# A decoder layer with expert retrieval: branches, first norm and scores by halves of the tokens, the second half laid between the gather slots of the first

## The chip, the cores and the metric

The kernel runs on one core of one Trainium2 chip. The metric is the device time of one execution in microseconds (us); a smaller time is better. The engines are PE (TensorE: matmuls, and its weight loads PEld), DVE (VectorE), ACT (ScalarE), POOL (GpSimd) and SP (SyncE, which here only issues DMAs). Sixteen DMA engines move data between DRAM and SBUF.

## What is computed

A decoder layer on 1024 tokens of width 1024. Cut to what matters here:

```python
h = x @ w_in                                   # q, k, v, p (pool, 512 wide), g (gates, 2048 wide)
o = rms_norm(diff_attention(q, k, v))          # 8 heads
attn_branch = o @ w_attn_proj
pooled = trailing_means(p) - p                 # windows 2, 4, 8, 16 along the tokens
pool_branch = (pooled @ pool_w * pool_scale) @ w_pool_proj
g_attn, g_pool = split(sigmoid(g + b_gate))
mix = (g_attn * attn_branch + g_pool * pool_branch) @ w_out
y = layer_norm(ALPHA * x + mix)
s = einsum(y @ peer_wq, sub_keys)              # 8 heads x 2 halves x 128 keys
top16 of each half, top16 of the 256 sums, idx = row * 128 + col, gate = softmax
act = gelu(u[idx] . y);  ffn = sum(gate * act * v[idx])     # 128 experts for each token
out = layer_norm(ALPHA * y + ffn)
```

Each token fetches 128 rows of u and v, chosen by its own scores: 1024 x 128 rows of 8 KB, 1.07 GB in all.

## The kernel before

Four stages follow one another, each closed by a barrier: `build_attention`, `build_branches`, `build_first_norm`, `build_peer`.

*Attention* (unchanged) leaves `xT_hi` and `xT_lo` (x turned, as a rounded part and the rest; every product of the first three stages is made of three fp32r matmuls of such parts) and `oT` in SBUF.

*Branches.* 20 blocks of `w_in` (4 for the pool branch, 16 for the gates) are loaded one by one. ACT makes the high part of a weight (L659), POOL the low part (L636), PE does two groups of 24 matmuls of 512 columns (one for each half of the tokens), ACT takes each out of PSUM (L671, or with the sigmoid L686). DVE does the pool branch's window sums for all 1024 tokens. Then 8 blocks of `w_branch` (ACT L699, POOL L647) are multiplied with `oT` and the pool result, 72 matmuls a block, and DVE gates and adds them (L768, L773, L778).

*First norm.* `w_out` is loaded and split (ACT L931, DVE L961), then 8 tiles of 128 tokens: 48 matmuls, residual and statistics on DVE (L971, L975), the power on POOL (L914), scaling on ACT (L936), gain and offset on DVE (L986, L988), store of y to DRAM, and 8 transposes into `yT`.

*Retrieval.* PE first multiplies query weights and keys into `km` (L1405), once for all tokens. The scores of a tile are then 32 plain fp32 matmuls (L1413). A tile has 128 **slots**, one gathered row for each of the 128 tokens: POOL issues the indirect DMA into a ring of 8 buffers (L1138), after PE has used the buffer's last content; DVE multiplies the u half with y and sums (L1364); ACT makes the gelu, the coefficient and a diagonal matrix, for a pair of slots at a time (L1183, L1187, L1193, 4 diagonal buffers); PE adds the v half by two fp32 matmuls (L1424). Beside the slots run the search of the head two ahead on DVE (`retrieve`, in 17 steps, `STEPS_AT` says how many at which slot), PE's scores of the next tile (one matmul each second slot, slots 17 to 79), and the last norm of the tile before. Each engine's order is written out by hand; DMAs queue on SP in program order.

Of the kernel before, what the change touches and what calls it, by code (L numbers as in the profile page):

```python
# [6 lines left out]

# [565 lines left out]

def build_branches(nc, ctx, w_in, pool_w, pool_scale, b_gate, w_branch, xT, oT, merged):
    at = Place(nc)
    pad = [at(f"pad{i}", 96 + 5 * i, [P, PAD + T]) for i in range(3)]
    pooled = [at(f"pooled{s}", 111 + 4 * s, [P, T], F32R) for s in range(2)]
    pw_raw = at("pw_raw", 119, [P, PG, P])
    pw = [at(f"pw{s}", 121 + 2 * s, [P, PG, P], F32R) for s in range(2)]
    count = at("count", 125, [P, PAD])  # L580
    icount = at("icount", 125.25, [P, PAD], I32)
    gates = at("gates", 96, [P, 2 * DC, T])
    pm_all = at("pm", 160, [P, PG, T])
    pm = [at("pm_hi", 32, [P, PG, T], F32R), at("pm_lo", 160, [P, PG, T], F32R)]
# [128 lines left out]
    def _(dve):  # L713
# [7 lines left out]
        for g, window in enumerate(WINDOWS):  # L721
# [7 lines left out]
            if g:  # L729
                dve.wait_ge(pooled_hi, g)  # L730
# [762 lines left out]
```

## Time and profile before

| | us |
|---|---|
| median of 3 runs | 3882.21 (3880.28 to 3883.63) |
| the profiled execution, whole time | 3879.75 |
| its span, first to last instruction | 3877.9 |
| attention | 0 to 667 |
| branches | 667 to 1070 |
| first norm | 1070 to 1184 |
| `km`, first scores, first searches | 1184 to 1257.6 |
| gathers issued | 1257.6 to 3848 |

The share of busy time of an engine is a mean over stages with different limits, so it is read by stage. A row of the grouped instructions gives their count, busy time, mean duration and the idle time before them. A row of the chain of waits names what the end was waiting for at that time. Matmul records of plain fp32 come in two for each instruction.

### The profile page before, as it was taken

To read this page: it belongs to the slowest core of one execution; us is meant where nothing else is said; L and a number is where in the kernel's file an instruction comes from. 1 tells how busy PE (TensorE), PEld (TensorE's weight loads), DVE (VectorE), ACT (ScalarE), POOL (GpSimd) and SP (SyncE) were. 2 spreads that over 40 slices of the span, in tenths; PEclk is the share of its full clock that TensorE was granted. 3 is DMA by queue.
4 is the path that set the end of the run, shared out by engine and by line. 5 is a ranking of instruction groups with operands and counts; after the bars stand their busy time and mean duration, and the time that the engine had idled before them with its cause. 6 is when DMAs were issued, how large, how long until landed. Compare 5 with 4: busy or idle time off the path is not lost.

```text
span 3877.9 us, 34466 instructions
## 1 busy us (share of the span) xinstructions
PE 3182.2 (82%) x9592; PEld 1687.1 (44%) x9592; DVE 2309.9 (60%) x5793; ACT 1233.1 (32%) x3644; POOL 1313.6 (34%) x1262
## 2 busy tenths in 40 slices
PE   7888886898987897788788788778878877877776
PEld 5767664687875333233233233323323323332222
DVE  4555555302252766766666667676677666767764
ACT  2333333222032333333333333333333333333332
POOL 2122111122200434444444444444444444444442
PEclk9989896999999999999999999999999999999999
DMA  2000000111034999999999999999999999999997
GB/s 83 17 23 22 22 11 9 42 46 48 32 130 132 409 421 421 420 419 414 418 418 417 419 414 419 414 415 417 415 415 417 416 415 416 419 416 415 413 417 331
DMA packets 166191, 1142.02 MB, mean 294 GB/s; under 512 B 19344, under 2 KB 19344, under 8 KB 34832
## 3 DMA queue, kind: packets, MB, share of 16 engines
q0 software_dynamic: 147456, 1073.81, 67.0%
q1 hardware_dynamic: 17856, 66.34, 5.0%
q8 instruction: 53, 0.87, 0.1%
q14 instruction: 106, 0.87, 0.1%
q10 hardware_dynamic: 720, 0.13, 0.0%
HBM read 1131.82 MB, written 8.39 MB: 294 GB/s over the span
## 4 chain that ended last, share of the span: by engine, by line
DMA 45%; PE 14%; DVE 5%; issue 3%; ACT 3%; POOL 0%; SPq 0%; POOLq 0%; ACTq 0%; DVEq 0%
DMA ring<-uv,idx 44%; PE r_o L1424 12%; DVE ring L1364 4%; ACT diag L1193 1%; DMA wq<-wqT 1%; PE r_s L1413 1%; ACT gel L1183 1%; ACT coef L1187 1%; PE r_s L1405 1%; POOL ring L1138 0%; DVE yn_e L1342 0%; DVE yn_e L1338 0%; DVE dot L1364 0%; DVE topi L1237 0%; DVE s L1238 0%
## 5 line engine op out<-in xcount | busy, mean ns | idle before, releaser
L1424 PE MATMUL r_o<-ring,diag 128*128 128x512 f32 x4096 | 1914.4, 611 | 492.8 <-ACT diag L1193 467.0
L1364 DVE CUSTOM_DVE_ANT_0 ring<-ring,ytok 128x1024 f32<-128x1024 f32 x1024 | 1253.7, 1224 | 774.0 <-DMA ring<-uv,idx 771.3
L1138 POOL DMA_INDIRECT ring<-uv,idx x1024 | 1083.4, 1058 | 1573.5 <-PE r_o L1424 1455.6
L1424 PEld LDWEIGHTS r_o<-ring,diag 128*128 128x128 f32 x4096 | 746.0, 192 | 1661.3 <-ACT diag L1193 861.7
L1183 ACT ACTIVATE gel<-dot 128x2 f32<-128x2 f32 x512 | 104.1, 203 | 1723.2 <-DVE dot L1364 1723.2
L1193 ACT ACTIVATE diag<-ident,coef 128x128 f32<-128x128 f32 x1024 | 347.4, 386 | 0.0
L66 PE MATMUL j_ps<-xT_hi,wa 128*128 128x512 f32 x768 | 258.4, 409 | 18.5 <-DVE xT_lo L354 18.5
L1413 PE MATMUL r_s<-km,yT 128*128 128x512 f32 x512 | 256.5, 592 | 0.8 <-ACT km L1155 0.8
L1187 ACT ACTIVATE coef<-gel,gate 128x1 f32<-128x1 f32 x1024 | 245.9, 287 | 16.8
L66 PE MATMUL b_ps<-xT_hi,wb 128*128 128x512 f32 x640 | 200.0, 393 | 12.8 <-POOL wb L636 10.1
L249 POOL TENSOR_SCALAR st_a<-st_a 128x1 f32<-128x1 f32 x64 | 12.2, 191 | 487.8 <-ACT sq L304 487.8
L66 PEld LDWEIGHTS j_ps<-xT_hi,wa 128*128 128x128 f32 x768 | 150.0, 195 | 60.6 <-issue 20.0
L66 PE MATMUL j_ps<-xT_lo,wa 128*128 128x512 f32 x384 | 154.9, 403 | 0.0
L316 ACT ACTIVATE e<-e,st_a 128x256 f32<-128x256 f32 (+7 forms) x128 | 98.3, 769 | 169.3 <-DVE st_a L430 169.3
L1413 PEld LDWEIGHTS r_s<-km,yT 128*128 128x128 f32 x512 | 97.2, 190 | 122.9 <-issue 121.9
L66 PEld LDWEIGHTS b_ps<-xT_hi,wb 128*128 128x128 f32 x640 | 121.8, 190 | 39.2 <-POOL wb L636 10.3
L66 PE MATMUL s_ps<-k,q 64*128 64x512 f32 (+2 forms) x576 | 109.1, 408 | 26.3 <-DVE st_a L425 26.2
L66 PE MATMUL b_ps<-xT_lo,wb 128*128 128x512 f32 x320 | 125.7, 393 | 0.0
L755 DVE TENSOR_TENSOR oT_lo<-oT,oT_hi 128x1024 fp32r<-128x1024 f32 x8 | 11.5, 1504 | 180.7 <-ACT oT_hi L703 180.7
L636 POOL TENSOR_TENSOR wb<-wb_raw,wb 128x1024 fp32r<-128x1024 f32 x20 | 48.2, 2410 | 187.0 <-ACT wb L659 187.0
L425 DVE CUSTOM_DVE_ANT_0 e<-s_ps,bias 128x512 f32<-128x512 f32 (+2 forms) x192 | 98.8, 553 | 7.0 <-DVE bias L413 2.7
L541 PE MATMUL o_ps<-v,aT 128*128 128x256 f32 x576 | 96.8, 323 | 3.2 <-DVE aT L400 3.2
(164 smaller groups left out, 2953.7 us busy)
## 6 DMA issues: line engine op xcount, KB each, us to landing
ring<-uv,idx POOLq DMA_INDIRECT x1024
wa_raw<-w_in SPq DMA_DIRECT2D x24, 512.0 KB, 3.6
wb_raw<-w_in SPq DMA_DIRECT2D x20, 512.0 KB, 3.6
wq<-wqT SPq DMA_DIRECT2D x16, 512.0 KB, 3.7
wc_raw<-w_branch SPq DMA_DIRECT2D x8, 768.0 KB, 4.2
x_raw<-xT SPq DMA_DIRECT2D x8, 512.0 KB, 9.5
wo_raw<-w_out SPq DMA_DIRECT2D x8, 512.0 KB, 7.4
xs<-x SPq DMA_DIRECT2D x8, 512.0 KB, 3.6
```

Source lines behind the costliest of these rows:

```text
L66: ins = nc.tensor.matmul(out, l(lhs[a]), r(rhs[b]), start=first and n == 0, stop=last and n == 3 * len(pairs) - 1)
L316: nc.scalar.activation(e[:, wh, 0:KEYS[s]], e[:, wh, 0:KEYS[s]], ACT.Exp, bias=nmx[:, wh:wh + 1], accum_out=den[:, wh:wh + 1]).then_inc(e_ ...
L425: nc.vector.tensor_tensor_reduce(e[:, wh, c * HALF:c * HALF + n], s_ps[i % 3][:, 0:n], bias[:, start:start + n], SCALE, -3.0e38, ALU.add, ...
L541: ins = nc.tensor.matmul(o_ps[:], part[:, i_a % 2, b * P:(b + 1) * P], v_both[u if tile >= 0 else 1 - u][:, :, 4 * c + b, :], start=c == 0 ...
L636: nc.gpsimd.tensor_tensor(w[r][1][:], w_raw[:], w[r][0][:].bitcast(F32), ALU.subtract).then_inc(w_split, 1)
L1138: nc.gpsimd.indirect_dma_start(out=ring[t % RING][:], out_offset=None, in_=uv, in_offset=bass.IndirectOffsetOnAxis(ap=idx[:, slot:slot + 1 ...
L1183: nc.scalar.activation(gel[:, slot:slot + GROUP], dot[:, slot:slot + GROUP], ACT.Gelu).then_inc(gelu_out, 1)
L1187: nc.scalar.activation(coef[:, slot + j:slot + j + 1], gel[:, slot + j:slot + j + 1], ACT.Copy, scale=gate[:, h, e:e + 1]).then_inc(coef_r ...
L1193: nc.scalar.activation(diag[(t + j) % DIAGS][:], ident[:], ACT.Copy, scale=coef[:, slot + j:slot + j + 1]).then_inc(diag_ready, 1)
L1364: nc.vector.tensor_tensor_reduce(ring[r][:, 0:D], ring[r][:, 0:D], ytok[n % 2][:], 1.0, 0.0, ALU.mult, ALU.add, dot[:, slot:slot + 1]).the ...
L1413: ins = nc.tensor.matmul(s_ps[b][:], yT[:, c, n * P:(n + 1) * P], km[:, c, b * HALF:(b + 1) * HALF], start=c == 0, stop=c == DC - 1)
L1424: ins = nc.tensor.matmul(o_ps[n % 2][half][:], diag[t % DIAGS][:], ring[t % RING][:, D + half * HALF:D + (half + 1) * HALF], start=slot == ...
```

## The change

After attention, everything is one block, `build_rest`, and everything between attention and retrieval is done for 512 tokens at a time (`stage(g)`, g = 0, 1) by smaller buffers. Stage 0 runs ahead of the gathers. Stage 1 is woven into the slots of tiles 0 to 3: after slot t every engine calls `advance(t)`, which emits those pieces of stage 1 whose number is at most t. The numbers:

```diff
+BASES = (-4000, 88)
+T_X, T_UNIT, UNIT_LEN = 0, 16, 6
+T_O = T_UNIT + UNIT_LEN * UNITS + 1
+T_BRANCH, BRANCH_LEN = T_O + 14, 8
+T_W = T_BRANCH + BRANCH_LEN * DC + 1
+T_NORM, NORM_LEN = T_W + 12, 12
+T_SCORE, HEAD_LEN = T_NORM + NORM_LEN * (GT + 1) + 4, 16
+def score_at(g, h):
+    if g == 0:
+        return HEAD_LEN * h - 62
+    return BASES[g] + T_SCORE + HEAD_LEN * h
```

So stage 1 loads its x at slot 88, does 20 units (a block of `w_in` times 512 tokens, 24 matmuls, 6 slots each) in slots 104 to 223, the 8 branch blocks (36 matmuls, 8 slots each) in 239 to 302, `w_out` from 304, four norm tiles (48 matmuls, 12 slots each) from 316, and its scores, a head each 16 slots, from 380 to 508. Of stage 0's scores the first 3.9 heads stand ahead of slot 0, the others in slots 2 to 66.

The scores no longer use `km`: queries are made for 512 tokens (8 fp32 matmuls of 512 columns for each of the 16 half heads), then compared with the keys (4 matmuls of 128 columns). They are stored to DRAM (`s_scr`, 512 KB a head) and read back by tile and head (128 KB, 64 times). `oT` goes through DRAM too (`o_scr`), x is loaded and split again for each half, and all weights of the stages (`w_in` blocks, `w_branch`, `w_out`, keys, query weights) are loaded twice. `w`, `wc` and the query weights have two buffers each, `mt`, `xs` and `zn` one.

The waits that the prediction speaks of:

```diff
+        def load_unit(g, i):                        # SP
+            u = UNITS * g + i
+            if u >= 2:
+                sp.wait_ge(unit, u - 1)
+            sp.dma_start(w_raw[u % 2][:], a["w_in"][FIRST_BLOCK + i]).then_inc(w_in[u % 2], 16)
...
+            def high(i):                            # ACT
+                u = UNITS * g + i
+                act.wait_ge(w_in[u % 2], 16 * (u // 2 + 1))
+                nc.scalar.activation(w[u % 2][0][:], w_raw[u % 2][:], ACT.Copy).then_inc(w_hi, 1)
...
+                yield unit_at(g, i + 1)
+                act.wait_ge(unit, u + 1)
...
+                    nc.scalar.activation(gates[:, j], ps[u % 2][:], ACT.Sigmoid, bias=bg[:, j:j + 1]).then_inc(evac, 1)
+                if i + 2 < UNITS:
+                    yield unit_at(g, i + 1) + 1
+                    high(i + 2)
...
+                yield branch_at(g, n + 1)           # DVE
+                dve.wait_ge(c_unit, 2 * c + 2)
+                nc.vector.tensor_tensor(gates[:, n + DC], gates[:, n + DC], ps[2 * (c % 2) + 1][:],
+                                        ALU.mult).then_inc(gated, 1)
...
+            if slot % TOPK == 13 and k + 3 < RH * TT:   # SP: s_scr to SBUF
+                search_in(k + 3)
```

**ACT, between two slot pairs of a gate unit.** Before, the rows of a slot pair stand alone (`gel`, two `coef`, two `diag`):

```order
L1193 ACTIVATE diag_6745<-ident,coef 128x128 [waits r_summed,r_coef_ready]
L1183 ACTIVATE gel<-dot 128x2 [waits r_dotted]
L1187 ACTIVATE coef<-gel,gate 128x1 [waits r_gelu_out]
L1187 ACTIVATE coef<-gel,gate 128x1
L1193 ACTIVATE diag_6742<-ident,coef 128x128 [waits r_summed,r_coef_ready]
L1193 ACTIVATE diag_6743<-ident,coef 128x128 [waits r_summed,r_coef_ready]
```

In the change, a sigmoid out of PSUM, the high part of a weight and two table loads stand between two pairs (slot 104 + 6k and the next one, then the pair behind):

```order
L1084 ACTIVATE diag_4931<-ident,coef 128x128 [waits r_summed,r_coef_ready]
L961 ACT_TABLE_LOAD
L961 ACTIVATE gates<-w_ps,bg 128x512 [waits r_unit]
L943 ACTIVATE wb_4870<-wb_raw_4861 128x1024 [waits r_w_in0]
L1074 ACT_TABLE_LOAD [waits r_gate_ready]
L1074 ACTIVATE gel<-dot 128x2 [waits r_dotted]
L1078 ACTIVATE coef<-gel,gate 128x1 [waits r_gelu_out]
L1078 ACTIVATE coef<-gel,gate 128x1
L1084 ACTIVATE diag_4928<-ident,coef 128x128 [waits r_summed,r_coef_ready]
```

The diagonals of the next pair now stand behind the wait for a weight load (`r_w_in0`).

**PE, slots of tile 0.** Before, one score matmul follows each second slot (two `r_o` rows are a slot):

```order
L1424 MATMUL r_o<-ring_6727,diag_6742 128x512 [waits r_diag_ready]
L1424 MATMUL r_o<-ring_6727,diag_6742 128x512
L1424 MATMUL r_o<-ring_6728,diag_6743 128x512 [waits r_diag_ready]
L1424 MATMUL r_o<-ring_6728,diag_6743 128x512
L1413 MATMUL r_s<-km,yT 128x512
```

In the change, where one unit ends and the next begins, three or six fp32r matmuls (`w_ps`) follow each slot:

```order
L1428 MATMUL w_ps<-xh,wb_4872 128x512
L1428 MATMUL w_ps<-xl,wb_4872 128x512
L1428 MATMUL w_ps<-xh,wb_4873 128x512
L1553 MATMUL r_o<-ring_4912,diag_4928 128x512 [waits r_diag_ready]
L1553 MATMUL r_o<-ring_4912,diag_4928 128x512
L1428 MATMUL w_ps<-xh,wb_4870 128x512 [waits r_evac,r_w_split]
L1428 MATMUL w_ps<-xl,wb_4870 128x512
L1428 MATMUL w_ps<-xh,wb_4871 128x512
L1428 MATMUL w_ps<-xh,wb_4870 128x512
L1428 MATMUL w_ps<-xl,wb_4870 128x512
L1428 MATMUL w_ps<-xh,wb_4871 128x512
L1553 MATMUL r_o<-ring_4913,diag_4929 128x512 [waits r_diag_ready]
```

The next unit's weights must be split by the slot at which the last unit ends.

**DVE, where a branch block ends (slot 255).** The rows of before have nothing between products (`ring,dot`) but search steps. In the change the gating stands between them:

```order
L1389 ISA ring_4919,dot<-ring_4919,ytok_4939 128x1024 [waits r_row_in7]
L1389 ISA dot 128x1
L1333 TENSOR_SCALAR gate<-gate,esum 128x16 [waits r_inverted]
L1192 TENSOR_TENSOR gates<-gates,w_ps 128x512 [waits r_c_unit]
L1389 ISA ring_4912,dot<-ring_4912,ytok_4938 128x1024 [waits r_row_in0,r_y_in0]
```

The product of slot 256 now stands behind the end of PE's work of slot 254.

## Rows read from the trace of the kernel before

**Rows 1.** The page: busy time by engine, and the DMA share in 40 slices.

```profile
PE 3182.2 (82%) x9592; PEld 1687.1 (44%) x9592; DVE 2309.9 (60%) x5793; ACT 1233.1 (32%) x3644; POOL 1313.6 (34%) x1262
...
DMA  2000000111034999999999999999999999999997
```

**Rows 2.** Windows: us, busy us of PE, PEld, DVE, ACT, POOL (instructions), PEclk, DMA, GB/s.

```profile
743.00:926.00 183.00, 177.49 (x774) 146.54 (x774) 2.27 (x2) 49.78 (x60) 36.10 (x15) 0.98 0.13 42
...
1070.00:1184.00 114.00, 99.19 (x448) 80.34 (x448) 63.12 (x88) 34.91 (x40) 4.49 (x9) 0.93 0.33 120
...
2300.00:2600.00 300.00, 245.32 (x532) 96.54 (x530) 206.62 (x524) 98.04 (x328) 125.90 (x119) 0.99 1.01 415
```

**Rows 3.** The chain of waits in the gathers: start us, us, what.

```profile
1240.10 27.75 PE r_s L1413 x64
...
1300.38 13.59 DMA ring<-uv,idx
1316.33 3.71 PE r_o L1424 x8
```

**Rows 4.** Source rows of the gathers: duration ns min/median/max, first and last start us.

```profile
L1138 POOL DMA_INDIRECT ring<-uv,idx x1024: 932/944/1997, 1257.6 to 3847.8; - x171
```

**Rows 5.** DMA issues: KB each, median us from issue to landing.

```profile
wb_raw<-w_in SPq DMA_DIRECT2D x20, 512.0 KB, 3.6
...
wc_raw<-w_branch SPq DMA_DIRECT2D x8, 768.0 KB, 4.2
...
y_scr<-y SPq DMA_DIRECT2D x8, 512.0 KB, 2.6
...
out<-yn_e SPq DMA_DIRECT2D x8, 512.0 KB, 7.6
```

**Rows 6.** Timeline, end of attention, first weights, first product of the branches.

```profile
666.95 0.30 PE L521 MATMUL t_ps<-ident,on 128*128 128x128 f32 x1 [2.38 <-ACT on L310]
677.32 0.80 PE L66 MATMUL b_ps<-xT_hi,wb 128*128 128x512 f32 x1 [10.06 <-POOL wb L636]
```

**Rows 7.** Groups by line: busy us, mean ns; idle before and its releaser.

```profile
L659 ACT ACTIVATE wb<-wb_raw 128x1024 fp32r<-128x1024 f32 x20 | 21.1, 1053 | 8.1 <-DMA wb_raw<-w_in 8.1
...
L699 ACT ACTIVATE wc<-wc_raw 128x1536 fp32r<-128x1536 f32 x8 | 11.9, 1486 | 91.3 <-PE b_ps L66 91.3
...
L768 DVE TENSOR_TENSOR gates<-gates,b_ps 128x512 f32 x16 | 11.0, 687 | 64.0 <-PE b_ps L66 64.0
...
L686 ACT ACT_TABLE_LOAD x7 | 9.0, 1283 | 28.2 <-PE b_ps L66 28.2
```

**Rows 8.** Source rows: POOL's low parts, and a DVE row that ran beside one.

```profile
L636 POOL TENSOR_TENSOR wb<-wb_raw,wb x20: 2337/2387/2538, 674.9 to 901.2; 128x1024 fp32r<-128x1024 f32 x20
...
L647 POOL TENSOR_TENSOR wc<-wc_raw,wc x8: 3437/3913/7633, 923.3 to 1036.3; 128x1536 fp32r<-128x1536 f32 x8
...
L741 DVE TENSOR_TENSOR pad<-pad,count x4: 163/170/2233, 692.9 to 739.7; 128x2 f32<-128x2 f32 x1, 128x4 f32<-128x4 f32 x1, 128x8 f32<-128x8 f32 x1, 128x16 f32<-128x16 f32 x1
```

**Rows 9.** Timeline: a first-norm tile on DVE, a second search's ends, a slot pair.

```profile
1092.27 0.69 DVE L971 SCALAR_TENSOR_TENSOR z<-xs,mix 128x512 f32<-128x512 f32 x1 [4.28 <-PE mix L66]
...
1098.16 1.23 DVE L988 TENSOR_TENSOR y<-y,gb 128x1024 f32<-128x1024 f32 x1
...
1257.38 0.48 DVE L1232 MAX8 top<-s 128x8 f32<-128x128 f32 x2
...
1266.87 0.28 DVE L1296 TENSOR_SCALAR gate<-best 128x16 f32<-128x16 f32 x1
...
1613.01 0.20 ACT L1183 ACTIVATE gel<-dot 128x2 f32<-128x2 f32 x1 [3.66 <-DVE dot L1364]
...
1614.07 3.70 PE L1424 MATMUL r_o<-ring,diag 128*128 128x512 f32 x8 [1.11 <-ACT diag L1193]
```

**Rows 10.** Groups of the gathers, 2300 to 2600 us: DVE's products.

```profile
L1364 DVE CUSTOM_DVE_ANT_0 ring<-ring,ytok 128x1024 f32<-128x1024 f32 x118 | 144.5, 1225 | 89.1 <-DMA ring<-uv,idx 89.1
```

More of the change, by code:

```diff
@@ L1105, in _, with store @@
             if n >= 2:
                 sp.wait_ge(joined, 2 * n - 2)
+            sp.wait_ge(y1_out, 16 * (n + 1))
             sp.dma_start(ytok[n % 2][:], y_scr[n]).then_inc(y_in[n % 2], 16)
-            if n >= 2:
-                sp.wait_ge(ready, n - 1)
-                sp.dma_start(out[n - 2], yn[:]).then_inc(stored, 16)
-                sp.wait_ge(stored, 16 * (n - 1))
-                sp.sem_inc(freed, 1)
-        for n in range(TT - 2, TT):
+        def store(n):
             sp.wait_ge(ready, n + 1)
@@ new lines, in _ @@
+        advance = woven(stage_chain(stage))
+        for h in range(3):
+            advance(stored_at(0, h))
+            search_in(h)
+        tokens_in(0)
+        for slot in range(LAST_SLOT):
+            n, k = slot // SLOTS, slot // TOPK
+            advance(slot)
+            if slot % TOPK == 13 and k + 3 < RH * TT:
+                search_in(k + 3)
+            if slot % SLOTS == 20 and n + 1 < TT:
+                tokens_in(n + 1)
+            if slot % SLOTS == 60 and n:
+                store(n - 1)
@@ L1120, in _ @@
+        store(TT - 1)
+        sp.wait_ge(stored, 16 * TT)
     @block.gpsimd
@@ L1194, in coefficients @@
                                      scale=coef[:, slot + j:slot + j + 1]).then_inc(diag_ready, 1)
-        for b in range(4):
-            copy_scores(0, b)
+        act.sem_inc(yn_ready, 1)
+        advance = woven(stage_chain(stage))
+        advance(-1)
         for g in range(LEAD):
@@ L1427, in spread @@
             ins.then_inc(summed, 1)
-        for b in range(4):
-            for c in range(DC):
-                score(0, b, c)
+        advance = woven(stage_chain(stage))
+        advance(-1)
         for n in range(TT):
@@ L1434, in _, with stage_chain, final_pad @@
                 spread(n, slot)
-                k = slot // 2 - 8
-                if n + 1 < TT and slot % 2 and 0 <= k < 4 * DC:
-                    score(n + 1, k // DC, k % DC)
+                advance(SLOTS * n + slot)
+def stage_chain(stage):
+    return itertools.chain(*(stage(g) for g in range(NG)))
+def final_pad(i):
+    return 2 - i % 2
 def program(nc, a, out):
```

1082 lines of the change are left out of this document (591 added, 491 removed).

## The prediction

> **What bounds the kernel now.** I read the page first. The DMA share is at 9 from the thirteenth slice to the end, while PE is the busiest engine over the whole span [rows 1]. So there are two kernels: 1258 us that wait for compute, and a gather stage. In a window of the gathers PE is busy 245 of 300 us, DVE 207, ACT 98, but the DMA engines all of it, at 415 GB/s [rows 2]. The chain of waits there repeats 13.6 us of DMA and 3.7 us of PE (two slots) [rows 3]: the ring's rows queue at the DMA engines, five deep. Gathers are issued from 1257.6 to 3847.8 us, 1023 intervals, 2.532 us a slot [rows 4]. A slot is 1.05 MB, 2.53 us at 415 GB/s: the bandwidth is the bound, and no order of the engines beats it. Ahead of it PE is busy 97% of 743 to 926 us [rows 2]. What can be gained is the time before 1257.6; what can be lost is that slots come slower than 2.532.
>
> **Prices.** An fp32r matmul of 512 columns is 177.5 us / 768 = 0.231 us [rows 2]. A plain fp32 one is 27.75 / 32 = 0.867 us (64 records, two for each) [rows 3], so PE's share of a slot is 1.73 us and its slack 0.80. A slot pair needs 1.06 us from the gelu to PE's start [rows 9].
>
> **Part 1, the work ahead of the gathers.** It ran 590 us, from 667.0 [rows 6] to 1257.6 [rows 4]. Now, with half the tokens:
> - Start: PE began 10 us after attention [rows 6]. SP now first saves `oT` (4.2 MB), loads the last norm's vectors (1 MB) and x again (2.4 MB): 7.6 MB, 18 us. 28 us.
> - 20 units of 24 matmuls, 5.5 us each. A buffer's cycle is unit, load 3.6 [rows 5], high part 1.05 [rows 7], low part 2.39 [rows 8], and 0.5 of semaphores: 13.1 us for two units, so PE waits. 20 x 6.6 + 2 for the pool products: 134 us.
> - `oT` back (2 MB, about 7 us), the first `w_branch` block behind it (3), high 1.49 [rows 7], low 3.9 [rows 8] and semaphores: 17 us.
> - 8 branch blocks: 36 x 0.231 = 8.3, load 4.2 [rows 5], 1.49, 3.9, 0.5: 18.4 for two, 74 us.
> - `w_out`: 4 MB before the first half product is done, 17 us, as all of it must land at 1.25 us a block after 4.
> - Norm: rest of the first tile 5.5, three times 11.1 + 2.5 (the single `mt` is copied and split between tiles), the chain from residual to y 7.1 [rows 9], turning 4: 57 us.
>
> That is 327 us: yT of the first half stands at 994. A half head of queries is 8 x 0.867 = 6.9 us and its comparison 0.9. The first head's scores are complete after three queries and two comparisons (22.6), are stored (2.6 [rows 5]) and read (about 3), and searched in 9.6 [rows 9]: first gather at 994 + 39. But the first product needs `ytok`, and SP loads that behind the store and the reading of the third head: 54 + 3 + 1 + 3.6 = 62. PE's first slot stands behind 3.9 heads (59) and gets its diagonal at 65. The eight rows have long landed (20 us), so 9 us of DMA are lost: the gathers effectively start at 994 + 48 = 1042. **Saved: 216 us.**
>
> **Part 2, what the gathers now carry.** DMA first. Stage 1 and the later half of stage 0's scores move 50.5 MB in slots 0 to 508 (`w_in` 10.5, `w_branch` 6.3, `w_out` 4.2, x, `oT` and pool weights 4.5, keys and query weights 13, scores stored 6.8, the norm's x, y and vectors 5.2), and the scores are read back by 64 x 128 KB, 8.4 MB more. 59 MB at 415 GB/s are 142 us. That is the least the gathers grow by.
>
> Then PE. In units a slot is 1.73 + 4 x 0.231 = 2.65 us, in branches 1.73 + 4.5 x 0.231 = 2.77, in scores 1.73 + 0.867 + 0.11 = 2.71: each over 2.532, about level with the DMA's new need (2.53 + 0.21 to 0.25). So neither has slack, and a wait in an engine's order is not made up.
>
> The largest such wait is **ACT's in a gate unit**. Let a unit end on PE at time 0, with the last matmul of its sixth slot. The load of the unit after next starts then (SP waits for `unit`), and ACT evacuates, then waits for that same load at once. PE has diagonals for two more slots: 2 x 1.73 + 9 x 0.231 = 5.5 us. ACT: landing, high part 1.05, table load 1.28 [rows 7], the pair's 1.06, semaphores 0.3. The landing is 3.6 in quiet; beside saturated gathers a store of the same size took 7.6 against 2.6 [rows 5], so 8.6 is the other end. I take 6, nearer the loaded row, as gathers run at 80% of the time then. ACT is ready at 9.7, PE lost 4.2: a unit is 15.9 + 4.2 = 20.1 against 15.2 before, +4.9. With the two ends +2.6 and +7.5. Over 16 units: **+78** (42 to 120). The 4 pool units have no table loads: +3.3 each, +13.
>
> The Trainium skill (DMA: Bandwidth & Descriptors, Queues, rings and completion order) says that each DMA engine goes round-robin between queues by packet; by it a small load doesn't queue behind five gathers, and the landing would be an estimated 5 us, the term +62. The trace agrees in that 7.6 is far below the gathers' own 13.6.
>
> **DVE's in a branch block.** Let B be a block's first slot. DVE's second gating stands behind the product of slot B+8 and waits for PE's work of slot B+7, when PE has only slot B+8 left to do (2.77). DVE: gating 0.69 [rows 7], product 1.3 [rows 10], search steps 0.8, the sum 0.75, product 1.3, then ACT 1.2: 6.1. PE loses 3.4, a block takes 22.0 + 3.4 against 20.3: 8 x 5.1 = **+41**.
>
> **Norm tiles**: 12 x 1.73 + 11.1 + 2.3 for the turning = 34.1, and about 5 of such waits (the power on POOL stands behind a gather's issue; the next residual behind PE's turning): 39 against 30.4, 4 x 8.6 + 3 = **+37**.
>
> The rest goes by DMA volume or PE's sum, whichever is more: scores of stage 1, 128 slots x 0.25 = 32; of stage 0, 66 x 0.25 = 16, and 7 because a head's scores pass DRAM twice just before DVE wants them; x +8; `oT` and first branch weights +12; `w_out` +15; reading scores in the other slots, 1 KB pieces, +16.
>
> Sum: 78 + 13 + 41 + 37 + 32 + 23 + 8 + 12 + 15 + 16 = **+275**. Searches, products, gelu and PE's diagonals are the same count; the km stage is gone (within part 1), and the end behind the last gather is unchanged.
>
> **Total**: 3877.9 - 216 + 275 = 3937 span, 3939 the execution; the profiled one stood 2.5 under the median, so 3941.
>
> **Rivals.**
> A, *cover holds, DMA volume decides*. If loads land in 3.6 and the two-slot reserves of ACT and DVE hide the waits, only 142 us and some 10 for the ends of stages remain: 3882 - 216 + 152 = 3818. For: the averages fit within 0.1 us a slot; the ring holds 20 us of rows, and PE has 0.8 of slack a slot in 100 of the 512. Against: the diagonals are only four, and in order; the ring's depth doesn't help PE. The waits that I add in units, branches, norm tiles and early scores beyond the DMA volume are some 115 us; with a third of them left it gives 3856. 0.29 with that, all faster.
> B, *the ends meet*: 3875 to 3890, 0.06.
> C, the forecast, slower, 3890 to 3985: 0.48.
> D, *POOL's low parts block DVE*. A DVE row of two columns took 2233 ns instead of 163 beside a low part, and one of POOL's took 7633 instead of 3437 beside DVE [rows 8]. 28 low parts now fall among the products; if each delays a product by 2.4 us that PE waits for, +67: 4008. It decides where DVE's lead over PE is under 2.4 us. For: the rows. Against: a low part is placed between two of ACT's waits, where DVE is ahead. 0.17, with landings at 8.6 (+42) in it. The Trainium skill (SBUF — State Buffer, on the shared port pair) has this as an exclusive lock for the whole instruction between GpSimd and DVE operations with two SBUF inputs; by that rule it would be this rival, and the trace agrees with it.
> That the change doesn't do what it says I leave out: the listing shows the pieces at the slots named.
>
> **Numbers.** Likeliest 3941. The parts of A below 3795 and of D above 4015, and what no case names, hold about 0.18 together: range 3795 to 4015. About 0.2% is what a measurement of this kernel can tell from no change: faster 0.29, same 0.06, slower 0.65. The forecast's own range is 3890 to 3985.
>
> **What would show it.** First gather near 1033 and first slot near 1059; more than 20 us off there moves all. In the 20 units of stage 1, slots of 3.3 us with PE idle on ACT's diagonals, ACT idle on `wb_raw`, and DMA near 80%; if DMA stays at its full share and slots take 2.75, A is right. In branches, PE idle 3 to 4 us once in eight slots, released through DVE. `wb_raw` landings of 5 to 7 us. DVE products of 3 us and more beside POOL rows mean D. Past slot 508 slots of 2.55. I am wrong if PE's fp32 and fp32r matmuls cost more when mixed, or if the unit's wait is hidden.

## The result: slower, and by more than forecast

The changed kernel takes 4087.5 us (median of 4, 4080.2 to 4093.1) against 3881.2 (3879.5 to 3883.6) for the kernel before: a ratio of 1.053, 95% interval 1.0512 to 1.0548. The forecast was 3941, slower; the measured time lies above its range. The profiled execution has a span of 4078.4 us, 141 more than the 3937 of the prediction's sum.

The page after, its lines of busy time and of the DMA engines in 40 slices of 102 us:

```profile
PE 3253.5 (80%) x9592; PEld 1744.6 (43%) x9592; DVE 2349.1 (58%) x5856; ACT 1317.9 (32%) x3737; POOL 1420.0 (35%) x1288
...
DMA  2000002223688988789999899999999999999998
```

Against [rows 1] the DMA engines come to work two slices earlier, but then stand at 7 and 8 where they stood at 9. That is the whole case: the gathers start early and run slowly. The source row of the gathers (durations in ns, first and last start):

```profile
L922 POOL DMA_INDIRECT ring<-uv,idx x1024: 932/943/2003, 1045.7 to 4048.2; - x171
```

[rows 4] had 1257.6 to 3847.8. The first product on DVE began at 1077.5 (before 1270.7), the last at 4061.7 (3861.3): 193 us won ahead, 394 lost in the 1023 slots. I measured each stretch by the starts of DVE's products, one for each slot, beside the same slots of the kernel before:

| slots | what is laid there | more than before, us | forecast |
|---|---|---|---|
| 0 to 88 | scores of the first half | 54.9 | 23 |
| 88 to 104 | x | 12.1 | 8 |
| 104 to 128 | pool units | 20.5 | 13 |
| 128 to 224 | gate units | 111.5 | 78 |
| 224 to 239 | `oT`, first branch weights | 19.9 | 12 |
| 239 to 304 | branch blocks | 41.1 | 41 |
| 304 to 316 | `w_out` | 9.7 | 15 |
| 316 to 380 | norm tiles | 47.7 | 37 |
| 380 to 508 | scores of the second half | 64.4 | 32 |
| 508 to 1023 | reading of scores | 11.8 | 16 |
| sum (unrounded) | | 393.5 | 275 |

Three terms carry most of the miss: the gate units (+33) and the two stretches of scores (+32 each); the front gave 23 us less than forecast.

**A gate unit**, timelines of PE and of ACT (start us, us, engine, line, what; in brackets the idle time before and who ended it):

```profile
1580.23 1.88 PE L1553 MATMUL r_o<-ring,diag 128*128 128x512 f32 x4
...
1587.59 3.78 PE L1553 MATMUL r_o<-ring,diag 128*128 128x512 f32 x4 [4.78 <-ACT diag L1084]
1590.38 1.42 PE L1428 MATMUL w_ps<-xh,wb 128*128 128x512 f32 x1
...
1592.44 2.06 PE L1553 MATMUL r_o<-ring,diag 128*128 128x512 f32 x4
```

```profile
1577.33 0.69 ACT L961 ACTIVATE gates<-w_ps,bg 128x512 f32<-128x512 f32 x1 [4.45 <-PE w_ps L1428]
1584.16 1.06 ACT L943 ACTIVATE wb<-wb_raw 128x1024 fp32r<-128x1024 f32 x1 [6.14 <-DMA wb_raw<-w_in]
1585.23 1.28 ACT L1074 ACT_TABLE_LOAD   x1
1586.53 0.20 ACT L1074 ACTIVATE gel<-dot 128x2 f32<-128x2 f32 x1
```

ACT takes the unit out at 1577.3 and stands 6.1 us at the load of the unit after next; the high part and the table load follow, the gelu comes at 1586.5, and PE has been idle for 4.8 us. This is the prediction's chain link by link. Then comes what it lacks: the two sums behind the gap take 3.78 us instead of 1.88, and the product behind them 1.42 instead of 0.80. PE comes out of the gap at half its rate. The next evacuation is at 1600.75, so this unit is 23.4 us, against 20.1 forecast. The mean of the 16 gate units is 15.2 + 111.5 / 16 = 22.2 us: PE's gap is 4.5 us in the mean, and in five of them only 2.2 to 3.3. Windows over the gate units and over slots past 508 (us, busy us of PE, PEld, DVE, ACT, POOL, PEclk, DMA share, GB/s):

```profile
1550.00:1750.00 200.00, 156.01 (x412) 84.65 (x410) 102.94 (x243) 76.96 (x172) 83.40 (x62) 0.87 0.80 303
...
2750.00:4048.00 1298.00, 967.30 (x2054) 378.13 (x2052) 879.45 (x2220) 414.81 (x1393) 547.13 (x513) 0.98 1.01 417
```

The granted clock is 0.87 in the first and 0.98 in the second.

**The scores.** DVE's waits in the whole trace (total us, times, longest), and those in 2250 to 2750, the second half's scores:

```profile
DVE top L1257 <- DMA s<-s_scr: 199.9, 17, 33.4
DVE esum L1328 <- ACT gate L1059: 91.0, 48, 14.8
```

```profile
DVE top L1257 <- DMA s<-s_scr: 73.9, 8, 11.7
```

The 33.4 is the first head's, ahead of the gathers; 14.4 more is the second head's, at 1059.9, also ahead of them. The other 152.1 us fall on 15 heads between the gathers. Before, the scores stayed in SBUF and there was no such load. SP now asks for a head's rows at slot 13 of 16, in order behind the query weights that wait for PE, and the rows then take 10 us and more. One such head on SP, DVE and PE:

```profile
2551.26 0.38 SPq L842 DMA_DIRECT2D s<-s_scr  x1
```

```profile
2564.93 0.49 DVE L1257 MAX8 top<-s 128x8 f32<-128x128 f32 x2 [11.68 <-DMA s<-s_scr]
```

```profile
2568.82 3.76 PE L1553 MATMUL r_o<-ring,diag 128*128 128x512 f32 x4 [7.31 <-ACT diag L1084]
```

Issue to use is 13.7 us, DVE is idle for 11.7 of them, PE for 7.3, and it comes back slowly again. The landings of the page after:

```profile
wb_raw<-w_in SPq DMA_DIRECT2D x40, 512.0 KB, 5.7
...
wc_raw<-w_branch SPq DMA_DIRECT2D x16, 768.0 KB, 8.6
wo_raw<-w_out SPq DMA_DIRECT2D x16, 512.0 KB, 9.3
s_scr<-s_out SPq DMA_DIRECT2D x16, 512.0 KB, 10.1
```

[rows 5] had 3.6 and 4.2 for the first two, ahead of all gathers. These medians of the page mix both halves. For the same kernel by windows, ahead of the gathers (0 to 1040 us) and then between them (1300 to 2100 us; the stored scores 2200 to 2760):

```profile
wb_raw<-w_in SPq DMA_DIRECT2D x20, 512.0 KB, 3.3
wc_raw<-w_branch SPq DMA_DIRECT2D x8, 768.0 KB, 4.4
```

```profile
wb_raw<-w_in SPq DMA_DIRECT2D x20, 512.0 KB, 7.4
wc_raw<-w_branch SPq DMA_DIRECT2D x8, 768.0 KB, 8.9
```

```profile
s_scr<-s_out SPq DMA_DIRECT2D x7, 512.0 KB, 12.1
```

### The profile page after: what moved, and what is told of

It reads as the page before. It is cut to its first block, busy times and chain, and to the rows that moved or that the text cites. A ratio compares the mean times of both kernels' runs of the same rounds, so it can differ in the third digit from the quotient of the medians.

```text
span 4078.4 us, 34054 instructions
## 1 busy us (share of the span) xinstructions
PE 3253.5 (80%) x9592; PEld 1744.6 (43%) x9592; DVE 2349.1 (58%) x5856; ACT 1317.9 (32%) x3737; POOL 1420.0 (35%) x1288
## 4 chain that ended last, share of the span: by engine, by line
PE 35%; DMA 32%; DVE 6%; ACT 5%; issue 4%; POOL 1%; SPq 1%; DVEq 0%; POOLq 0%
DMA ring<-uv,idx 22%; PE r_o L1553 22%; PE w_ps L1428 8%; PE w_ps L1539 4%; DMA wb_raw<-w_in 4%; DVE ring L1389 4%; DMA s<-s_scr 3%; DMA s_scr<-s_out 1%; ACT diag L1084 1%; ACT gel L1074 1%; ACT wb L943 1%; DMA wc_raw<-w_branch 1%; ACT coef L1078 1%; PE w_ps L1522 1%; POOL wb L895 1%
## 5 line engine op out<-in xcount | busy, mean ns | idle before, releaser
L1553 PE MATMUL r_o<-ring,diag 128*128 128x512 f32 x4096 | 2019.9, 631 | 601.9 <-ACT diag L1084 576.9
L1389 DVE CUSTOM_DVE_ANT_0 ring<-ring,ytok 128x1024 f32<-128x1024 f32 x1024 | 1270.5, 1241 | 682.0 <-DMA ring<-uv,idx 673.3
L1553 PEld LDWEIGHTS r_o<-ring,diag 128*128 128x128 f32 x4096 | 787.1, 199 | 1649.7 <-ACT diag L1084 833.0
L1428 PE MATMUL w_ps<-xh,wb 128*128 128x512 f32 x640 | 282.3, 488 | 40.3 <-POOL wb L895 40.2
L1539 PE MATMUL w_ps<-yT,wq 128*128 128x512 f32 x512 | 263.9, 616 | 4.7 <-DMA wq<-wq 4.1
L1428 PEld LDWEIGHTS w_ps<-xh,wb 128*128 128x128 f32 x640 | 125.4, 196 | 101.9 <-POOL wb L895 46.3
L1539 PEld LDWEIGHTS w_ps<-yT,wq 128*128 128x128 f32 x512 | 101.5, 199 | 133.2 <-issue 127.9
L1257 DVE MAX8 top<-s 128x8 f32<-128x128 f32 x128 | 31.0, 284 | 199.9 <-DMA s<-s_scr 199.9
L1428 PE MATMUL w_ps<-wo,mt 128*128 128x512 f32 x384 | 120.2, 455 | 26.6 <-DVE mt L1204 16.9
L1428 PE MATMUL w_ps<-xl,wb 128*128 128x512 f32 x320 | 128.5, 402 | 0.0
L895 POOL TENSOR_TENSOR wb<-wb_raw,wb 128x1024 fp32r<-128x1024 f32 x40 | 96.4, 2412 | 91.1 <-ACT wb L943 90.7
L1428 PE MATMUL w_ps<-oh,wc 128*128 128x512 f32 x256 | 109.4, 478 | 20.4 <-POOL wc L901 19.1
```

What stands on the lines that cost most here:

```text
L895: nc.gpsimd.tensor_tensor(w[u % 2][1][:], w_raw[u % 2][:], w[u % 2][0][:].bitcast(F32), ALU.subtract).then_inc(w_split, 1)
L1389: nc.vector.tensor_tensor_reduce(ring[r][:, 0:D], ring[r][:, 0:D], ytok[n % 2][:], 1.0, 0.0, ALU.mult, ALU.add, dot[:, slot:slot + 1]).the ...
L1428: ins = nc.tensor.matmul(out, lhs[l], rhs[r], start=first and i == 0, stop=last and i == 2)
L1539: ins = nc.tensor.matmul(ps[hp % 2][:], wq[hp % 2][:, c * P:(c + 1) * P], yT[:, c, :], start=c == 0, stop=c == DC - 1)
L1553: ins = nc.tensor.matmul(o_ps[n % 2][half][:], diag[t % DIAGS][:], ring[t % RING][:, D + half * HALF:D + (half + 1) * HALF], start=slot == ...
```

## The experiments

The theory after the result, called **W** below: each engine's order puts a wait for something late ahead of work that was ready, and PE pays for the idle time twice, by the gap and by the slow restart. Rival **V**: the DMA volume or PE's own added work sets the slots, and waits would only move. Each kernel had its times taken beside runs of the kernel before (medians 3878.7 to 3880.4).

### e1: the rows of scores are asked for 12 slots earlier

```diff
-            if slot % TOPK == 13 and k + 3 < RH * TT:
+            if slot % TOPK == (13 if k + 3 < RH else 1) and k + 3 < RH * TT:
```

> Edit: SP's read of a head's scores (s from s_scr) stands at slot 1 of its group of 16 instead of slot 13, for heads from the 8th on; nothing else moves. Theory W (waits in an engine's order): the read was issued only after SP's waits on PE, about one slot before DVE wanted it, and took 11 to 14 us; 12 of the 16 long waits of DVE (166 us in all) go, each also worth a slow restart of PE, so the slots 380 to 508 fall from 3.1 to about 2.8 us and the kernel to about 4005 (3980 to 4030). Theory V (volume: DMA bytes and PE's sum set the pace of the slots): the bytes and the matmuls are the same, so 4075 to 4100. Theory P (POOL's low parts block DVE): no change either.

Measured: 4038.6 us, ratio 1.0411 (1.0386 to 1.0437). DVE's waits for these rows fell from 199.9 to 103.5 us:

```profile
DVE top L1257 <- DMA s<-s_scr: 103.5, 7, 33.4
```

49 us gone, where I had looked for about 80, and the time lies above W's range (up to 4030). Slots 380 to 508 went from 64.4 to 27.9 over before, the norm tiles from 47.7 to 39.0; in the pool and gate units nothing went (24.6 and 115.8, from 20.5 and 111.5), though DVE waited for rows there too. That ACT's own wait, which sets those units, takes up the time that is won is argued, not shown; e3 below bears on it. W has the direction, but not the size.

### e2: ACT takes the next high part two slots later

```diff
-                    yield unit_at(g, i + 1) + 1
+                    yield unit_at(g, i + 1) + 3
                     high(i + 2)
```

> Edit: ACT makes the high part of the weight after next two slots later (unit slot 3 instead of 1); nothing else moves. Theory W: the load has 5 us more to land before ACT waits for it, so PE no longer idles 5 us in each of the 16 gate units and the 4 pool units, and doesn't restart slowly after it: a gate unit falls from 23.4 to 16.6 to 18 us, the kernel by 80 to 110 us, to about 3990. Theory V: same bytes and matmuls, 4075 to 4100. Theory P: the low part comes later and nearer to PE's need, so the same or slower.

Measured: 3986.6 us, ratio 1.0279 (1.0261 to 1.0296): 101 us for one number. The gate units went from 111.5 to 29.3 us over before, the pool units from 20.5 to 12.7. The same window as above:

```profile
1550.00:1750.00 200.00, 191.95 (x574) 108.19 (x573) 138.68 (x327) 108.87 (x245) 109.92 (x84) 0.98 1.00 410
```

The DMA share went from 0.80 to 1.00, the clock from 0.87 to 0.98. By V both would have stayed.

### e3: both

> Both edits together: reads of the scores early, high parts late. Theory W: the gains add, about 170 us, to 3915 (3880 to 3960), still slower than the kernel before, as branches, norm tiles and the first 66 slots keep their waits. Theory V and theory P: 4075 to 4100.

Measured: 3934.9 us, ratio 1.0138 (1.0121 to 1.0155). 49 + 101 = 150, measured 153: the gains add (W's range was 3880 to 3960), and part of what e1 lacked in the gate units is seen here, 21.4 us over before against 29.3 in e2.

### e4: a third of the second half's unit products

```diff
-        def triple(out, lhs, rhs, first, last):
-            for i, (l, r) in enumerate(((0, 0), (0, 1), (1, 0))):
+        def triple(out, lhs, rhs, first, last, count=3):
+            for i, (l, r) in enumerate(((0, 0), (0, 1), (1, 0))[:count]):
...
-                                 c == DC - 1)
+                                 c == DC - 1, 1 if g else 3)
```

> Edit: in the 20 units of stage 1 (slots 104 to 223) PE does one of the three matmuls of each product, 8 instead of 24 a unit, so part of the products is left out; all loads, splits and waits stay. PE's sum for a unit falls from 15.9 to 12.2 us. Theory W: the unit is set by the load's landing, high part, table, pair and four more slots: about 21.5 instead of 23.4 us, the kernel 40 us faster, 4045. Theory V by PE's sum: the units fall to the DMA's pace, 16.6 us, 110 us faster, 3975; by DMA bytes alone nothing changes.

Measured: 4023.1 us (2 runs), ratio 1.0371 (1.035 to 1.0392). PE's work for 20 units fell by 20 x 16 x 0.231 = 74 us, the time by 64: between the two theories, nearer to W's 4045 than to V's 3975. The gates still cost 67.6 us over before:

```profile
1550.00:1750.00 200.00, 140.61 (x312) 65.99 (x310) 117.66 (x269) 92.01 (x205) 93.76 (x69) 0.84 0.87 340
```

PE is busy 141 of 200 us here and its gathers still run at 340 GB/s: PE waits (`PE r_o <- ACT diag`, 59.4 us of the 200). Two thirds of the unit's matmuls gone bought less than ACT's two slots did.

### e5: the first half's scores 12 slots earlier too

The edits of e3, with

```diff
-        return HEAD_LEN * h - 62
+        return HEAD_LEN * h - 74
...
-            if slot % TOPK == 13 and k + 3 < RH * TT:
+            if slot % TOPK == 1 and k + 3 < RH * TT:
```

> The two edits of e3 (rows of scores asked for 12 slots earlier, ACT's next high part two slots later), and the scores of the first half 12 slots earlier too, so that all of their rows can be asked for 12 slots ahead. e3 ran at 3935, and its slots 0 to 66 took 54 us more than those of before; in 1077 to 1260 DVE waited 39.0 us in three times for rows of scores. Theory W (what is left there is again a wait in order, not work): the three quarters of a head that now come ahead of the first gather cost 0.75 x 15.5 = 12 us, and about 40 of the 54 us go: 3907 (3895 to 3920). Rival V (slots 0 to 66 are slow since TensorE and the DMA engines have the scores to do beside the gathers): 3935 + 12 - 10 = 3937 (3930 to 3950).

Measured: 3906.7 us, ratio 1.0064 (1.0047 to 1.0081), W's number. Slots 0 to 66 fell from 54.4 to 13.3 us over before, and DVE's longest waits in 1090 to 1260 are now

```profile
DVE ring L1389 <- DMA ring<-uv,idx: 58.1, 51, 2.6
DVE esum L1328 <- ACT gate L1059: 2.0, 4, 0.5
```

where the changed kernel had 48.1 us in four times for rows of scores (1077 to 1295, its slots 0 to 66). But slots 66 to 88 rose from 1.8 to 11.0: see e9.

### e6: DVE's steps of branches and norm 2 to 4 slots later

The edits of e3, with the following; the other steps of a norm tile (POOL's, ACT's, gain, offset, store) moved by 2 to 5 slots likewise.

```diff
-T_NORM, NORM_LEN = T_W + 12, 12
+T_NORM, NORM_LEN = T_W + 12, 16
...
-                yield branch_at(g, n) + 6
+                yield branch_at(g, n) + 9
...
-                yield branch_at(g, n + 1)
+                yield branch_at(g, n + 1) + 3
...
-                yield branch_at(g, n + 1) + 1
+                yield branch_at(g, n + 1) + 5
...
-                    yield norm_at(g, n + 1) + 1 + half
+                    yield norm_at(g, n + 1) + 3 + half
```

> The edits of e3, and in the second half's branches DVE takes its products 3 slots later after the matmuls that they read; in the norm DVE's, POOL's and ACT's steps stand 2 to 4 slots later and a tile has 16 slots instead of 12. In e3 the slots 239 to 304 took 45 us more than before, 316 to 380 38 us. Theory W (in-order waits that others of the engine's work stands behind: DVE's waits there were 62.7 us for matmuls of the branches and 57.9 us in the norm): half or more of the 83 us goes: 3890 (3875 to 3905). Rival P (the matmuls themselves, 576 of the branches and 768 of w_out beside the sums of the rows, are what these slots wait for; the waits only move): 3930 (3920 to 3940).

Measured: 3910.2 us, ratio 1.0074 (1.0058 to 1.0091): 25 us under e3, midway between W (45) and P (5, the matmuls themselves set these slots), outside both ranges. The branch slots went from 45.0 to 29.2, the norm's 316 to 380 from 38.4 to 10.8; 6 came back at `w_out` and 6 past slot 508. DVE waited 80.5 us for the branch products of the second half in the changed kernel (45.4 at L1189, 35.1 at L1192); in 1840 to 2250 us of e6 L1189 is no longer in the list, and of L1192 there is

```profile
DVE gates L1192 <- PE w_ps L1428: 7.9, 5, 2.4
```

so the waits were real, and a part of what they cost belonged to PE and DMA anyway.

### e7: all of these

> All edits of e5 and e6. Theory W, if the gains add: 3935 - 28 - 45 = 3862 (3845 to 3885), under the 3879 to 3884 of the kernel before. Rival (V and P, the work itself sets these slots): 3930 to 3950.

Measured: 3882.4 us (10 runs), ratio 1.0005 (0.9996 to 1.0015): no difference from the kernel before. From e3, e5 took 28, e6 25; 28 + 25 = 53 and 52.5 came. Windows over slots 0 to 66, the gate units, the branches, the norm and the late slots:

```profile
1084.00:1259.00 175.00, 165.90 (x428) 76.61 (x428) 115.11 (x308) 63.24 (x197) 71.87 (x64) 0.98 0.95 390
...
1448.00:1714.00 266.00, 256.92 (x762) 144.03 (x761) 196.88 (x447) 144.64 (x331) 150.70 (x111) 0.99 1.00 403
...
1767.00:1965.00 198.00, 178.22 (x525) 101.35 (x526) 141.49 (x318) 62.91 (x188) 99.02 (x70) 0.97 0.91 358
...
2010.00:2182.00 172.00, 159.03 (x448) 85.38 (x447) 127.85 (x316) 60.45 (x187) 71.08 (x65) 0.96 1.01 412
...
2538.00:3863.00 1325.00, 990.33 (x2141) 389.34 (x2140) 889.71 (x2240) 424.09 (x1422) 545.26 (x515) 0.99 1.01 414
```

In the gate units PE's own sum by the prediction's prices is 96 x 1.73 + 384 x 0.231 = 255 us, and it is busy 257: fp32 and fp32r matmuls cost no more when mixed. All but the branches have 0.95 or more of DMA share, so what is left of the 188 us that the slots still cost over before should be mostly bytes; e9 and e10 weigh that.

### e8: nothing laid between the gathers

```diff
-BASES = (-4000, 88)
+BASES = (-4000, -2000)
...
-        return HEAD_LEN * h - 62
+        return HEAD_LEN * h - 3000
```

> The changed kernel, but nothing is laid between the gathers: all scores of the first half and then the whole second half are done before the first gather. It separates what halving costs from what laying it between the gathers costs. From the rows of the changed kernel: five heads more at 15.5 us = 78 us, and a second half that alone takes 145 (units) + 76 (branches) + 85 (w_out and norm) + 8 x 15.5 (scores) + 15 (its first loads) = 445 us, so the first gather starts at about 1046 + 78 + 445 = 1569; from there the gathers take what they took before, 2590, and the kernel ends at about 4170 (4140 to 4210). Theory W (weaving does hide most of the second half, and waits give back a part): 4170, 80 over the changed kernel. Rival H (weaving hides nothing that matters, the changed kernel's 206 us over before are the price of doing the work twice in halves): 4087 or less.

Measured: 4211.5 us, ratio 1.0856 (1.0838 to 1.0874), 41 over W's number, just above its range, and far from H's: the first product came at 1579.3, and the slots took 21 us more than before (11 of them past slot 508). So the halves without weaving cost 309 us ahead of the first product over the kernel before; some 248 of the time ahead are 16 heads of scores at 15.5 us, which before mostly ran between the gathers. Laying work between the gathers took 502 us off the front (1579.3 to 1077.5) and put 372 back (393.5 less 21): it hid a quarter of what it moved. With both halves' scores done ahead, slots 0 to 88 are at the old pace (+1.5 us), though SP still reads every head's rows back at slot 13. From 1579 us on DVE never waits for them; its longest totals there are

```profile
DVE ring L1389 <- DMA ring<-uv,idx: 793.4, 850, 2.5
DVE esum L1328 <- ACT gate L1059: 24.0, 49, 0.6
```

So neither the way through DRAM nor slot 13 is what costs 10 us a head in the changed kernel. There SP stands behind waits for PE, beside stores and weights that are also under way; here SP has none of these and asks as soon as a buffer is free. Which of the two makes the wait, the order or the other transfers, e8 doesn't part; e1 shows that asking earlier takes most of it away.

### e9: only bytes added

The kernel of e7, with 56 loads of 512 KB that nothing reads:

```diff
+            if 560 <= slot < 1008 and slot % 8 == 5:
+                j = (slot - 560) // 8
+                if j:
+                    sp.wait_ge(extra_in, 16 * j)
+                sp.dma_start(w_raw[0][:], a["w_in"][FIRST_BLOCK + j % UNITS]).then_inc(extra_in, 16)
```

> The kernel of e7 (3882), and from slot 560 on, where nothing of the second half is left, every eighth slot a load of 512 KB of w_in into a buffer that nothing reads: 56 loads, 29.4 MB, nothing else added or changed. It measures the price of a byte beside the gathers by itself. Theory A (once no engine waits in order, the slots take what the DMA engines need; a slot is 1.05 MB in 2.53 us, 415 GB/s): 29.4 / 0.415 = +71 us, 3953 (3940 to 3965). Rival (the 2.53 us of a slot are set by the gathers' own descriptors or issue, with room for other queues beside them): 3882 to 3895.

Measured: 3951.4 us, 69 over e7. Slots 508 to 1023 grew by 70.7 us, forecast 71. The rate stays what it was, over more us (e9, then e7):

```profile
2682.00:3898.00 1216.00, 876.91 (x1792) 341.64 (x1791) 779.10 (x1977) 365.08 (x1231) 488.51 (x451) 0.96 1.01 415
```

```profile
2680.00:3826.00 1146.00, 841.19 (x1790) 326.69 (x1788) 778.15 (x1976) 364.75 (x1230) 480.85 (x451) 0.99 1.01 415
```

Beside these gathers a byte costs its full time at 415 GB/s. That fits the 9 us that came back in slots 66 to 88 in e5: with the waits gone the DMA engines are at their full share there (1.02 in e7) with x and the first weights to load.

### e10: begun earlier and spread wider

The kernel of e7, with `ytok`'s first load behind the first head's rows, and

```diff
-BASES = (-4000, 88)
+BASES = (-4000, 68)
-T_X, T_UNIT, UNIT_LEN = 0, 16, 6
+T_X, T_UNIT, UNIT_LEN = 0, 16, 7
...
-T_BRANCH, BRANCH_LEN = T_O + 14, 8
+T_BRANCH, BRANCH_LEN = T_O + 14, 9
```

> The kernel of e7, with the second half begun at slot 68 instead of 88, a gate unit spread over 7 slots instead of 6 and a branch block over 9 instead of 8, and the first tile's tokens loaded behind the first head's rows instead of the third's (8 us that DVE waits ahead of its first product). Theory W: what e7 keeps in slots 0 to 508 beyond the bytes is TensorE's own work crowded into too few slots (busy 256.9 of 266 us in the gate units at 403 GB/s, 178.2 of 198 in the branches at 358 GB/s against 415 to 420 elsewhere); spread out, 8 + about 20 us go: 3855 (3840 to 3870), faster than both kernels. Rival A (only bytes are left, e7's slots carry 50 to 60 MB more than those of before, and these cost the same wherever they stand): 3872 (3868 to 3878), the start alone.

Measured: 3867.4 us (8 runs, 3864.3 to 3870.8), ratio 0.9969 (0.9958 to 0.9979): faster than both kernels, by 0.3% over the one before, and 15 us under e7 (11 by the profiled spans). W's number was 3855 (3840 to 3870), A's 3872 (3868 to 3878): it lies at the upper end of W's range, 0.6 under A's, and in number it is nearer A, so it doesn't part the two. The `ytok` load gained nothing: the first product stands at 1083.3 (e7 1084.3), since DVE waits 16.1 us there for ACT's first exponent, which stands in ACT's order behind the scores. The gain is slots 68 to 508, 1262.9 us against 1273.5. Windows over the slots that hold products (e10, then the kernel before):

```profile
1083.00:3852.00 2769.00, 2298.98 (x5646) 1046.98 (x5647) 1900.67 (x4645) 983.07 (x2989) 1222.60 (x1055) 0.98 1.00 409
```

```profile
1271.00:3861.00 2590.00, 2101.57 (x4534) 829.33 (x4535) 1778.50 (x4527) 848.77 (x2839) 1082.46 (x1023) 0.99 1.01 416
```

2769 x 0.409 = 1133 MB against 2590 x 0.416 = 1077: 55 MB more, 133 us at 415 GB/s, of the 179 that the slots take longer. The other 46 are left to waits; no run says to which. One candidate is in the section on rivals below: DVE's products beside POOL's low parts.

### e11: the gaps of PE filled

The changed kernel, with

```diff
+                    if g and i >= NP + 3 and c == 2:
+                        pe.wait_ge(pm_scaled, NP * (g + 1))
+                        for _ in range(18):
+                            nc.tensor.matmul(ps[2][:], x_s[0][:, 0, 0:P], x_s[0][:, 0, :], start=True, stop=True)
```

> The changed kernel, with 18 fp32r matmuls more (18 x 0.231 = 4.2 us, into a bank that nothing reads) in each of the second half's last 13 gate units, placed where TensorE otherwise stands idle 4.8 us for ACT's diagonal; no wait is moved. In the changed kernel the sums behind such a wait took 3.78 us (4 records) and the next products 1.42 and 0.63 instead of 1.88, 0.80 and 0.39. Theory C (the idle time itself brings the slow restart: the engine comes back at half its rate, some 2.6 us a unit): with the gap filled the sums take 1.9 us again and a unit shrinks from 23.4 by up to 2.6: 13 x 2.6 = 34 us, 4087 becomes 4055 (4050 to 4070), and the granted clock of 1560 to 1740 us rises from 0.84 to 0.89 to above 0.93. Rival (the slow restart has another cause, such as the diagonal's or the rows' late arrival, and would stay; the added matmuls cost nothing or a little): 4085 to 4100.

Measured: 4071.2 us, ratio 1.0498 (1.048 to 1.0515). More work in PE's order made the kernel 16 us faster (13 by the two ratios), and the gate units have it: 96.8 us over before instead of 111.5. The time lies 1 us above C's range (4050 to 4070) and well under the rival's (4085 to 4100). Two units in a row on PE, and the window:

```profile
1570.05 4.27 PE L1461 MATMUL w_ps<-xh 128*128 128x512 f32 x18
1577.32 3.67 PE L1557 MATMUL r_o<-ring,diag 128*128 128x512 f32 x4 [3.00 <-ACT diag L1084]
...
1594.96 4.27 PE L1461 MATMUL w_ps<-xh 128*128 128x512 f32 x18
1600.65 1.98 PE L1557 MATMUL r_o<-ring,diag 128*128 128x512 f32 x4 [1.41 <-ACT diag L1084]
```

```profile
1550.00:1750.00 200.00, 186.54 (x594) 112.94 (x594) 109.76 (x268) 83.57 (x189) 88.06 (x64) 0.97 0.83 320
```

Where 1.41 us of idle time were left the sums took 1.98, where 3.00 were left 3.67, with the same diagonal waited for: the slow restart goes with the idle time, and not with the diagonal or the rows. The clock rose from 0.87 to 0.97. Half of theory C's 34 us came, as a part of the gaps stayed and ACT's wait for the load, which no matmul shortens, still sets the unit.

## Why the prediction was right and wrong

**The front** (saved 216, measured 193). The first gather came at 1045.7 (forecast 1033), the first slot at 1077.5 (1059). The work ahead was about 11 us longer than the 327 of the sum: PE began the first query at 1005.3 instead of 994. The half-head times held (7.8 us). What failed behind it is the term "54 + 3 + 1 + 3.6" for `ytok`: SP stored the third head's scores at 1061.5, could ask for its rows only at 1072.6, 11 us later instead of 3, and then for `ytok`, for which the first product waited 7.3 us:

```profile
1061.54 0.33 SPq L805 DMA_DIRECT2D s_scr<-s_out  x1
1072.62 0.33 SPq L842 DMA_DIRECT2D s<-s_scr  x1
1072.99 0.95 SPq L848 DMA_DIRECT2D ytok<-y_scr  x1
```

```profile
1077.54 1.23 DVE L1389 CUSTOM_DVE_ANT_0 ring<-ring,ytok 128x1024 f32<-128x1024 f32 x1 [7.33 <-DMA ytok<-y_scr]
```

In e10 that load is early, and ACT's first exponent takes its place as the last wait.

**Gate units** (+78, measured +111.5). The mechanism and its place were right, and e2 shows it by taking it away. The step that failed is "PE lost 4.2": in the unit shown the gap was 4.8, and the 2.6 us that follow it at half rate (sums 3.78 for 1.88, products 1.42 for 0.80 and the next two) were in no term. I listed the chain of releases and never asked in what state PE comes back. e11 shows that this part exists apart from the wait. The mean unit lost 7.0 us over before, against 4.9 in the sum.

The landing that I took at 6 us between 3.6 and 8.6 was 7.4 in the median of the second half's blocks, so this term was short too, by 1.4 us. The estimate of 5 us by the round-robin of queues (the Trainium skill, DMA: Bandwidth & Descriptors, Queues, rings and completion order) was too low: the block shown left ACT waiting until 6.8 us after the unit's end, and the loaded medians of `w_branch` and of the stored scores are 8.9 and 12.1.

**Scores** (+23 and +32, measured +55 and +64). Here the mechanism was missed. "The rest goes by DMA volume or PE's sum, whichever is more" is the sentence that failed: I priced bytes and matmuls, and gave the passage through DRAM 7 us, in the first half only. I didn't follow the reading through SP's order: at slot 13, three slots (7.6 us) ahead of its use, it stands behind SP's waits for PE, and in the head shown 13.7 us passed from issue to use. e8, where SP has no such waits, has none of DVE's either. e1 takes 36.5 of the 64.4 us away, and what it leaves, 27.9, is close to the 32 of the sum; e5 takes 41 of the 54 in slots 0 to 66.

**Branches** (+41, measured +41.1) and **norm tiles** (+37, +47.7): the norm tiles come to 39.0 in e1, so most of their excess was again the rows of scores. For the branches e6 shows that the branch waits were not all of it: with them nearly gone, 29 us of 45 stay. The sum named one mechanism for what has more than one cause, and its match was in part luck. What holds the rest no run separates; in e7's branches (1767 to 1965 us) there are bytes, PE's own sum, and

```profile
ACT wc L985 <- DMA wc_raw<-w_branch: 67.0, 6, 13.6
PE r_o L1553 <- ACT diag L1084: 19.8, 7, 4.1
```

**The rivals.** A, that bytes alone decide, was wrong for this kernel and comes nearer for what it becomes when mended: 133 of e10's 179 us in the slots are bytes, but its time is 3867 against A's 3818. D's mechanism is there by the sign that the prediction gave, products of 3 us and more beside POOL rows, but it is small in this kernel. 25 of the 1024 products ran beside one of POOL's low parts, with a mean of 2.01 us against 1.22 for the others, five of them 3.3 to 4.7 us; the mean of all is 1241 ns against 1224, 17 us of DVE's time, where D had 67 us of PE's. In the gate units most of this hides behind ACT's wait for its weights. Where it doesn't, PE stands through it (POOL, DVE and PE at one place of the branches):

```profile
1885.83 3.42 POOL L901 TENSOR_TENSOR wc<-wc_raw,wc 128x1536 fp32r<-128x1536 f32 x1
```

```profile
1885.63 4.72 DVE L1389 CUSTOM_DVE_ANT_0 ring<-ring,ytok 128x1024 f32<-128x1024 f32 x1
```

```profile
1891.45 5.38 PE L1553 MATMUL r_o<-ring,diag 128*128 128x512 f32 x6 [8.98 <-ACT diag L1084]
```

With the waits mended it grows: 26 such products with a mean of 2.63 us in e7, 27 with 2.77 in e10, 36.5 and 41.8 us more of DVE's time than at 1.22. How much of that is PE's too was not tested. The chance of faster, 0.29, rested on reserves of two slots hiding the waits; in the changed kernel they hid too little: ACT waited 154.8 us for blocks of `w_in`.

Small slips of the prediction, without weight: the DMA share is at 9 from the fourteenth slice, not the thirteenth; 3.9 heads at 15.6 us are 61 us, not 59; and a landing of 6 is the middle of 3.6 and 8.6, not nearer the loaded end.

## What to carry to other kernels

Work laid between the steps of a bandwidth-bound loop costs its bytes in full (e9). The rest of it comes near to free only if each of its waits stands where the thing waited for is long done: one number, two slots, was worth 101 us here (e2). Before such a change, list each in-order wait with what is queued behind it, on SP as well, and ask for loads a landing time earlier than the loaded trace shows, not the quiet one. And price a stall of PE at more than its length, since after 4.8 us of idle time the matmuls that followed ran at half their rate and cost 2.6 us more.

## What was not expected of the hardware

- PE behind 3.0, 4.8 and 7.3 us of idle time took 3.67, 3.78 and 3.76 us for two sums, behind 1.4 us 1.98 (usual 1.88). In the gathers of the changed kernel all 31 idle times of 4 us or more before such sums were followed by 3.24 to 3.78 us; of the shorter ones in the gate units, one of 3.24 us was followed by 1.98 and three of 3.20 to 3.29 us by 3.41 to 3.65. The granted clock of the gate units was 0.87, and 0.97 with idle time filled by useless matmuls. The Trainium skill (TensorE: Matmul & The Clock Gate, HAM oscillation — how this bites in real kernels) tells of waits for DMA that put PE back to the lower of its two clocks at each block; the trace agrees, for a wait on ACT's diagonal. That filling such a gap pays even in a kernel bound elsewhere (16 us) I had not expected.
- Stores and small loads beside the gathers take 7 to 12 us (512 KB of weights 7.4, 768 KB 8.9, 512 KB of scores stored 12.1), not the 3.3 and 4.4 of the same loads ahead of them, while their bytes cost only their share (56 loads, 29.4 MB, 70.7 us). Late, but not expensive: what is asked for early enough is cheap.
- DVE's two-input products take up to 4.7 us instead of 1.2 when they meet a POOL operation that splits weights (25 of them in the changed kernel, mean 2.01 us); the other 999 have a mean of 1.22 us.
